# Landing each weight chunk in two halves: a two-layer transformer and a hybrid layer on one core

## What is computed

```python
def swiglu(x, w_gate_up, w_down):
    g, u = jnp.split(x @ w_gate_up, 2, axis=-1)
    return (jax.nn.silu(g) * u) @ w_down

# layer 0
y = short_conv_mixer(rms_norm(h, g0), conv_w_in, conv_w, conv_w_out)
h = h + rms_norm(y, post0)
h = h + rms_norm(swiglu(rms_norm(h, f0), w_gate_up[0], w_down[0]), fpost0)
# layer 1: k, v = shared_kv(h); dilated attention; the same feed-forward
# second block: x @ w_in, attention and pooling branches, w_out, conv feed-forward
```

## Time and profile before

| | us |
|---|---|
| median of 3 runs | 1239.92 |
| the profiled execution's own time | 1239.94 |
| its span | 1238.0 |
| PE busy | 1159.1 (94%) |
| DVE busy | 727.2 (59%) |
| ACT busy | 584.2 (47%) |
| all DMA, mean rate over the span | 156 GB/s |

### The profile page before, as it was taken

One profiled execution on the slowest core, in us unless ns is written; L12 is line 12 of the kernel. 1 busy time (PEld: TensorE's weight loads), 2 busy tenths in 40 slices (PEclk: granted clock), 3 DMA queues, 4 the chain that ended last, 5 costly groups with the idle time before them and its releaser, 6 DMA issues.

```text
span 1238.0 us, 17037 instructions
## 1 busy us (share of the span) xinstructions
PE 1159.1 (94%) x6724; PEld 1033.6 (83%) x6724; DVE 727.2 (59%) x940; ACT 584.2 (47%) x738; POOL 63.4 (5%) x49
## 2 busy tenths in 40 slices
PE   5998999989888999999988999999899998899998
PEld 5996777778888999999966777788898897899987
DVE  3865454455755565566555445455665564888862
ACT  4435534354545444554445534454534373566550
POOL 0110000000000000000000000000020020122310
PEclk8998999999999999999999999999999999999999
DMA  6554455666265554435233565766516353455662
GB/s 202 185 193 151 155 165 175 211 219 202 54 165 136 153 152 104 128 96 130 102 127 108 164 193 156 241 208 170 136 57 184 111 183 121 156 185 172 212 221 75
DMA packets 211330, 193.70 MB, mean 156 GB/s; under 512 B 5529, under 2 KB 186829, under 8 KB 211277
## 3 DMA queue, kind: packets, MB, share of 16 engines
q1 hardware_dynamic: 211277, 192.95, 50.8%
HBM read 191.88 MB, written 1.05 MB: 156 GB/s over the span
## 4 chain that ended last, share of the span: by engine, by line
PE 50%; DMA 17%; DVE 14%; ACT 9%; issue 7%; SPq 2%; ACTq 0%; DVEq 0%
DVE w_lo L1545 10%; DMA raw<-in_ffn_w_gate_up 7%; PE ps L570 6%; PE ps L572 6%; PE ps L571 6%; DMA raw<-in_ffn_w_down 4%; ACT w_hi L1117 4%; PE ps L695 3%; PE ps L697 3%; PE ps L696 3%; PE ps L620 3%; PE ps L621 3%; PE ps L622 3%; DMA raw<-in_w_q 3%; PE ps L726 2%
## 5 line engine op out<-in xcount | busy, mean ns | idle before, releaser
L1545 DVE TENSOR_TENSOR w_lo<-raw,w_hi 128x2048 fp32r<-128x2048 f32 (+2 forms) x157 | 404.5, 2588 | 156.4 <-ACT w_hi L1117 156.4
L1117 ACT ACTIVATE w_hi<-raw 128x2048 fp32r<-128x2048 f32 (+2 forms) x157 | 338.3, 2156 | 321.8 <-DMA raw<-in_ffn_w_gate_up 125.9
L570 PE MATMUL ps<-x_hi,w_hi 128*128 128x256 f32 x656 | 187.9, 286 | 5.0 <-DVE w_lo L1545 5.0
L571 PE MATMUL ps<-x_lo,w_hi 128*128 128x256 f32 x656 | 186.2, 284 | 0.0
L572 PE MATMUL ps<-x_hi,w_lo 128*128 128x256 f32 x656 | 186.1, 284 | 0.0
L620 PE MATMUL ps<-w_hi,x_hi 128*128 128x512 f32 (+1 forms) x368 | 146.1, 397 | 1.0 <-DVE w_lo L1545 0.7
L622 PE MATMUL ps<-w_hi,x_lo 128*128 128x512 f32 (+1 forms) x368 | 143.1, 389 | 0.0
L621 PE MATMUL ps<-w_lo,x_hi 128*128 128x512 f32 (+1 forms) x368 | 143.1, 389 | 0.0
L570 PEld LDWEIGHTS ps<-x_hi,w_hi 128*128 128x128 f32 x656 | 126.6, 193 | 5.5 <-DVE w_lo L1545 5.4
L571 PEld LDWEIGHTS ps<-x_lo,w_hi 128*128 128x128 f32 x656 | 126.7, 193 | 0.1
L572 PEld LDWEIGHTS ps<-x_hi,w_lo 128*128 128x128 f32 x656 | 126.5, 193 | 0.0
(11 more groups left out here) (218 smaller groups left out, 1738.3 us busy)
## 6 DMA issues: line engine op xcount, KB each, us to landing
raw<-in_ffn_w_gate_up SPq DMA_DIRECT2D x88, 512.0 KB, 4.9
raw<-in_w_kv SPq DMA_DIRECT2D x48, 512.0 KB, 6.4
raw<-in_w_up SPq DMA_DIRECT2D x22, 1024.0 KB, 5.1
raw<-in_conv_w_in SPq DMA_DIRECT2D x12, 1024.0 KB, 5.1
raw<-in_ffn_w_down SPq DMA_DIRECT2D x8, 1536.0 KB, 7.3
raw<-in_w_q SPq DMA_DIRECT2D x24, 512.0 KB, 5.2
raw<-in_ffn_w_down SPq DMA_DIRECT2D x8, 1280.0 KB, 6.0
raw<-in_w_in SPq DMA_DIRECT2D x10, 1024.0 KB, 5.5
```

The costliest lines, as they stand in the source:

```text
L570: nc.tensor.matmul(o, wh[:, k0 + k, c], hi[:, k, :], start=(k == 0), stop=False)
L571: nc.tensor.matmul(o, wh[:, k0 + k, c], low, start=False, stop=False)
L1117: nc.scalar.activation(w_hi[:, s, 0:size], raw[:, r, 0:size], ACT.Copy)\
L1545: nc.vector.tensor_tensor(w_lo[:, s, 0:size], raw[:, r, 0:size], w_hi[:, s, 0:size], ALU.subtract)\
```

## The change

`raw` keeps its size but has four places of half the size. Each chunk is cut by K tiles (8 into 4 and 4, 6 into 3 and 3, 5 into 3 and 2, 4 into 2 and 2). Each half has its own place, its own DMAs, its own semaphore, its own copy on ACT and its own subtraction on DVE. `hi_ready` and `lo_ready` count halves: the load of a half waits for DVE's subtraction of the same half of chunk n-2, and PE still waits for both halves of a chunk. Pieces that were one DMA become two, but for the four chunks of `branches`, whose two pieces are the two halves already. The memory of `raw`, the four places of `w_hi` and `w_lo`, PE's program and the order of the other work stay.

```diff
--- before.py
+++ after.py
@@ -68,8 +68,20 @@
     def size(self, j):
         return self.kts[j] * self.cols
 
+    def part(self, j, h):
+        mid = (self.kts[j] + 1) // 2
+        return (0, mid) if h == 0 else (mid, self.kts[j])
+
+    def part_pieces(self, j, i, h):
+        a, b = self.part(j, h)
+        cut = [(max(k0, a), min(k0 + kn, b), k0, c0, cw, src) for k0, kn, c0, cw, src in self.pieces(j, i)]
+        return [(lo - a, hi - lo, c0, cw, src[:, lo - k0:hi - k0, :]) for lo, hi, k0, c0, cw, src in cut if hi > lo]
+
     def n(self, j, i):
         return i * 4 + (self.n0 + j)
+
+    def n2(self, j, i):
+        return i * 8 + 2 * (self.n0 + j)
 
 
 def build(nc, a, out):
@@ -97,7 +109,7 @@
 
 
         SLOT = 3072
-        raw = at("raw", [P, 2, SLOT], F32)
+        raw = at("raw", [P, 4, SLOT // 2], F32)
         w_hi = at("w_hi", [P, 4, SLOT], F32R)
         w_lo = at("w_lo", [P, 4, SLOT], F32R)
         h = at("h", [P, 2, D], F32)
@@ -243,20 +255,22 @@
             Phase("down2", 8, DOWN_KT, 512, down_pieces(down_w[2]), banked=False),
         ]
         by_name = {}
-        chunk_at, landed, per_slot = [], [], [0, 0]
+        chunk_at, landed, per_slot = [], [], [0, 0, 0, 0]
         for ph in phases:
             ph.n0 = len(chunk_at)
             by_name[ph.name] = ph
             for l in range(ph.count):
                 real = not (ph.empty_last and l % 4 == 3)
+                r = len(chunk_at) % 2 * 2
                 if real:
-                    per_slot[len(chunk_at) % 2] += 16 * len(ph.pieces(l % 4, l // 4))
-                landed.append(per_slot[len(chunk_at) % 2])
+                    for h_ in range(2):
+                        per_slot[r + h_] += 16 * len(ph.part_pieces(l % 4, l // 4, h_))
+                landed.append(per_slot[r:r + 2])
                 chunk_at.append((ph, l) if real else None)
         TOTAL = len(chunk_at)
 
 
-        raw_in = [sem(f"raw_in{s}") for s in range(2)]
+        raw_in = [sem(f"raw_in{s}") for s in range(4)]
         hi_ready = sem("hi_ready")
         lo_ready = sem("lo_ready")
         product_done = sem("product_done")
@@ -435,13 +449,18 @@
                 n, i = n + 4 * i, 0
             eng.wait_ge(emptied[n % 4], i + (used[n] + 1))
 
-        def raw_level(ph, j, i):
+        def raw_slot(ph, j, h_):
+            r = (ph.n0 + j) % 2 * 2 + h_
+            a, b = ph.part(j % 4, h_)
+            return r, raw[:, r, 0:(b - a) * ph.cols]
+
+        def raw_level(ph, j, i, h_):
 
             n = ph.n0 + j
             if isinstance(i, int):
-                return landed[n + 4 * i]
-            step = landed[n + 4] - landed[n]
-            return i * step + landed[n]
+                return landed[n + 4 * i][h_]
+            step = landed[n + 4][h_] - landed[n][h_]
+            return i * step + landed[n][h_]
 
         def next_chunk(ph, l):
 
@@ -487,11 +506,13 @@
         def _(sp):
             def load(ph, j, i):
                 n = ph.n(j, i)
-                if not isinstance(i, int) or n >= 2:
-                    sp.wait_ge(lo_ready, n - 1)
-                s = (ph.n0 + j) % 2
-                for k0, kn, c0, cw, src in ph.pieces(j, i):
-                    sp.dma_start(slot(raw, s, ph)[:, k0:k0 + kn, c0:c0 + cw], src).then_inc(raw_in[s], 16)
+                for part in range(2):
+                    if not isinstance(i, int) or n >= 2:
+                        sp.wait_ge(lo_ready, ph.n2(j, i) + (part - 3))
+                    r, flat_raw = raw_slot(ph, j, part)
+                    dst = flat_raw.rearrange("p (k c) -> p k c", c=ph.cols)
+                    for k0, kn, c0, cw, src in ph.part_pieces(j, i, part):
+                        sp.dma_start(dst[:, k0:k0 + kn, c0:c0 + cw], src).then_inc(raw_in[r], 16)
 
             sp.dma_start(ident[:], a["c_ident"]).then_inc(x_in, 16)
             for t in range(2):
@@ -548,7 +569,7 @@
         @block.tensor
         def _(pe):
             def ready(ph, j, i, bank=True):
-                pe.wait_ge(lo_ready, ph.n(j, i) + 1)
+                pe.wait_ge(lo_ready, ph.n2(j, i) + 2)
                 n = ph.n0 + j + (4 * i if isinstance(i, int) else 0)
                 if bank and (used[n] > 0 or not isinstance(i, int)):
 
@@ -763,7 +784,7 @@
                     if n == 0:
                         pe.wait_ge(v_stored, 8)
                         pe.wait_ge(o_split, 6)
-                    pe.wait_ge(lo_ready, w.n0 + j + 1)
+                    pe.wait_ge(lo_ready, w.n2(j, 0) + 2)
                     ins = tokens(w, j, t, range(4), Y_BANK[3][t][j], x_hi, x_lo, first=True)
                     if t == 1:
                         ins.then_inc(product_done, 1)
@@ -1109,13 +1130,15 @@
         def _(act):
             def split(ph, j, i):
 
-                n, s, r = ph.n(j, i), (ph.n0 + j) % 4, (ph.n0 + j) % 2
-                act.wait_ge(raw_in[r], raw_level(ph, j, i))
-                if not isinstance(i, int) or n >= 4:
-                    act.wait_ge(product_done, n - 3)
-                size = ph.size(j)
-                nc.scalar.activation(w_hi[:, s, 0:size], raw[:, r, 0:size], ACT.Copy)\
-                    .then_inc(hi_ready, 2 if ph.empty_last and j == 2 else 1)
+                n, s = ph.n(j, i), (ph.n0 + j) % 4
+                for part in range(2):
+                    r, src = raw_slot(ph, j, part)
+                    act.wait_ge(raw_in[r], raw_level(ph, j, i, part))
+                    if part == 0 and (not isinstance(i, int) or n >= 4):
+                        act.wait_ge(product_done, n - 3)
+                    a, b = ph.part(j, part)
+                    nc.scalar.activation(w_hi[:, s, a * ph.cols:b * ph.cols], src, ACT.Copy)\
+                        .then_inc(hi_ready, 3 if part and ph.empty_last and j == 2 else 1)
 
             def high(bi, t, r, k):
 
@@ -1538,12 +1561,15 @@
 
             def split(ph, j, i):
 
-                n, s, r = ph.n(j, i), (ph.n0 + j) % 4, (ph.n0 + j) % 2
+                s = (ph.n0 + j) % 4
                 two = ph.empty_last and j == 2
-                dve.wait_ge(hi_ready, n + (2 if two else 1))
-                size = ph.size(j)
-                nc.vector.tensor_tensor(w_lo[:, s, 0:size], raw[:, r, 0:size], w_hi[:, s, 0:size], ALU.subtract)\
-                    .then_inc(lo_ready, 2 if two else 1)
+                for part in range(2):
+                    r, src = raw_slot(ph, j, part)
+                    dve.wait_ge(hi_ready, ph.n2(j, i) + (part + 1))
+                    a, b = ph.part(j, part)
+                    c = slice(a * ph.cols, b * ph.cols)
+                    nc.vector.tensor_tensor(w_lo[:, s, c], src, w_hi[:, s, c], ALU.subtract)\
+                        .then_inc(lo_ready, 3 if part and two else 1)
 
             def low(bi, t, r, k):
```

## The result

The changed kernel takes 1198.11 us (median of 4 runs, 1197.05 to 1202.7), beside it the kernel before 1239.11 (4 runs): ratio 0.968, 95% interval 0.965 to 0.972, so it is faster by 2.8 to 3.5%. The forecast was 1201.0, the range 1191 to 1218. The profiled execution took 1197.06 us with a span of 1195.1; against the 1238.0 of before that is 42.9 us less.

The account below looks back on a forecast made before the run. Up stages were held by an 11.94 us loop through one landing place, PE needing 11.33. Waits 33.5 plus clock 6.0 less instructions 0.8 gave 38.7 off 1239.9: 1201 us, range 1191 to 1218.

Parts of the forecast that it names:

- The loop: Up stages, one unit through a landing place: 11.94 us falls to 10.3, under PE's 11.33, so PE becomes the bound.
- 1 transposes: PE's waits at L684 for mid_t in gate and up units: 16.0 us of 18.0 saved.
- 2 L620: PE's four waits at L620 for late chunks: 3.0 us of 3.4 saved.
- 3 attention, first steps: Waits at L695, L740 and L747 behind L1298 in attention's first steps: 8.0 us of 8.4 saved.
- 4 L654: Waits at the boundaries, behind DVE's split, including the end of down1: 2.4 us of 8.5 saved.
- 5 L855: Wait behind ACT's split at 891.15 and a root that DVE waits for: 2.5 us of 5.5 saved.
- 7 L584: PE's wait for the first chunk: ACT ends 0.85 us sooner, at a halved clock, 0.4 us of 6.8 saved.
- clock, the nine stretches: PE's 3.4 us stretches at 0.50 after the first 20 us: three go, two shrink, 6.0 us saved.
- more instructions: Second copies and subtractions for 157 chunks: hidden except at seven places of 0.12 us each, costing 0.8 us.
- Halves land no sooner: Rival on landing: the second half still lands 4.90 us after issue, saving only 26 us, 1214; chance 0.18.
- Slower, the DMA queue: Rival in up0 and up1: eight 256 KB DMAs per unit make the queue the bound, 1260 us; chance 0.04.
- Waits move on: Rival: PE's other partners become late and halved clock returns elsewhere, costing 5 to 8 us; no separate chance given.

Follow-up runs that it names:

- experiment 3: The changed kernel, but ACT's first copy of a chunk waits until both halves have landed: 1218.72 us, ratio 0.985.
- 4: The changed kernel, but both halves' loads wait until both halves of the chunk two before are subtracted: 1214.32 us, ratio 0.982.
- 5: The kernel before, with only ACT's order in gate and up units changed, silu and hidden_high ahead of the second split: 1217.92 us, ratio 0.984.
- experiment 9: The changed kernel with silu and hidden_high moved ahead of the second split in ACT's body of up0 and up1: 1197.57 us, ratio 0.965.
- experiment 11: The changed kernel, but PE starts on the first half at five w_lo waits, at two also on a pair's first chunk alone: 1184.24 us, ratio 0.958.
- experiment 6: The changed kernel, but in up0 and up1 both halves are asked for together and ACT waits for both: 1229.41 us, ratio 0.993.
- experiment 2: The kernel before, each load cut into DMAs of half the K tiles, with one wait for both, copy and subtraction whole: 1254.22 us, ratio 1.015.
- 7: The changed kernel, but up0 and up1 fully as in the kernel before, with whole chunks and uncut DMAs: 1215.16 us, ratio 0.980.
- 8: The kernel before with halves in up0 and up1 alone, every other phase as before: 1218.12 us, ratio 0.982.

## Why the prediction was right, by its steps

**The loop**: forecast 2.35 + 0.71 + 4.0 + 0.10 + 1.05 + 2.10 = 10.3 us; the rows above give 2.36 for the two halves (mean 1.218 each, starting 1.14 apart), 0.76 to the last DMA, 4.18 to the copy, 1.06 and 2.12: 10.48. The one estimate in it was the landing: 4.0 and 0.10 to the copy, 4.18 measured for the two; PE became the bound, as said. Experiments 3 and 4 show that both overlaps were needed for that, 5 that the loop's path went through the silu.

**The sum**, each with 0.16 per wait as in the prediction, forecast and measured:

| term | forecast | measured, from the waits before and after |
|---|---|---|
| 1 transposes | 16.0 | 15.1 - 0.5 + 16 x 0.16 = 17.2 |
| 2 L620 | 3.0 | 3.4, none left |
| 3 attention, first steps | 8.0 | 3.1 + 2.3 + 2.4 + 4 x 0.16 = 8.4 |
| 4 L654 | 2.4 | 2.3 + 2 x 0.16 = 2.6 |
| 5 L855 | 2.5 | 2.0 |
| 6 L747 behind L1391 | 1.2 | 0.6 |
| 7 L584 | 0.4 | 2.3 |
| clock, the nine stretches | 6.0 | 3.9 |
| clock, first 20 us | not counted | 1.5 |
| more instructions | -0.8 | -0.2 |
| sum | 38.7 | 41.7 of 42.9 |

The clock's number: after the first 20 us the windows at 0.50 hold 29.8 us of PE's busy time before and 22.0 after (the sums of the view of windows over all of them), and half of the 7.8 is saved; in the first 20 us they hold 2.9 before and none after. Of the five stretches that were to go or shrink, those at 102, 351, 795 and 935 us are gone; the one after L855 stayed. One at 609.2 is new, behind a wait of 1.82 us at L761, and that in the last boundary is 6.8 long instead of 3.4. The wait at L761 is no longer than it was before the change (also 1.82, at 639.14, with the clock at 1.00 after it), so the record does not show why the clock fell there. The -0.2 is what L591 and L625 grew by; more is hidden in what the other rows already count. That the total came so close is in part luck: the waits gave 3.0 more than forecast and the start's clock 1.5, the nine stretches 2.1 less.

**The step that was mis-sized** is term 7. I had counted half a copy at ACT's end (0.85) and put it down to 0.4. What I overlooked stands in the timelines of ACT, before and after:

```profile
11.38 1.91 ACT L1117 ACTIVATE w_hi<-raw 128x2048 fp32r<-128x2048 f32 x1 [2.26 <-DMA raw<-in_conv_w_in]
```

```profile
8.88 2.23 ACT L1140 ACTIVATE w_hi<-raw 128x1024 fp32r<-128x1024 f32 x2
```

The first half of the first chunk is there when ACT asks for it, 2.5 us before the one DMA of 1 MB was. The second half sets the pace, as the chains of work show, before and after (start, us, what):

```profile
3.07 8.29 DMA raw<-in_conv_w_in
```

```profile
3.53 6.50 DMA raw<-in_conv_w_in
```

It lands at 10.03 where the whole chunk landed at 11.36. That is 1.33 us sooner, which I had left out, and ACT's last copy is 0.85 shorter (1.06 for 1.91), which I had in it: together the 2.2 by which PE starts sooner. The first product starts at 15.07 instead of 17.18, after PE has stood for 4.46 us instead of 6.80. The clock of the first 20 us changed as well. Before, after, and in experiment 9:

```profile
13.30:20.10 6.80, 2.92 (x13) 2.92 (x14) 6.05 (x8) 6.42 (x13) 0.00 (x0) 0.50 0.46 126
```

```profile
13.30:20.10 6.80, 5.03 (x29) 5.04 (x30) 6.17 (x12) 5.83 (x10) 0.00 (x0) 1.00 0.72 203
```

```profile
13.30:20.10 6.80, 4.43 (x20) 4.43 (x21) 6.76 (x13) 5.87 (x11) 0.00 (x0) 0.57 0.69 192
```

0.50 before and 1.00 after. The prediction had left this stretch out of its clock, and the shorter wait does not explain it: in experiment 9 PE stood for the same 4.46 us and was granted 0.57, in experiment 11 for 3.46 and 0.75, and in experiment 6 it stood for 5.42 and kept 1.00. So the 1.5 us in the table are no gain that the change is shown to bring, and the other clock row, read from one execution of each kernel, carries some of the same doubt.

**The rivals.** *Halves land no sooner*: false, 256 KB land in 4.2 where 512 KB took 4.9; this is the page's issue part after, then before:

```profile
raw<-in_ffn_w_gate_up SPq DMA_DIRECT2D x176, 256.0 KB, 4.2
```

```profile
raw<-in_ffn_w_gate_up SPq DMA_DIRECT2D x88, 512.0 KB, 4.9
```

*Slower, the DMA queue*: eight DMAs fit in a unit of 11.4 us, but the mechanism exists. In the unit shown it has its place in the issues and not in the bytes: experiment 2 lost 16 us, and there the last DMA goes out 1.1 us later and lands 0.5 sooner. In the change the later issues are hidden, since the first half's DMAs go out while DVE subtracts the second. The rule of the Trainium skill ("DMA: Bandwidth & Descriptors", Measured), to batch to 1 MiB, points the way that experiment 2 went; it does not hold for the change itself, where a smaller DMA is released and used sooner. The 2.6 us estimated from that page for 256 KB ("Anatomy of one DMA", a fit to DMAs issued from GpSimd, where these are issued from SP) stand against 4.2 measured with others in flight, and eight of them take 11.4 us or less and not 21, so they overlap. *Waits move on* happened in small, as halved clock that came back elsewhere: the stretch at 609.2 gave back nearly 1.8 us. DVE was 743.6 and ACT 603.2 us busy, where near 745 and near 615 were forecast; in the last up projection DVE stood at 18.27 of 20 us, beside 18.39 before.

**What the expectations had wrong**: experiment 2 by 4 us; experiment 3 by 8 us, since I counted the copy's overlap and not that the landing is longer; experiment 6 by 3 us, its edit changed more than it was read to; experiment 11 by 4 us to the fast side, about what the halved clock gave it. Of the last 1.2 us of the 42.9, 0.9 are small waits that the table leaves out: 0.4 at L794, which is gone, 0.1 at L707, and 0.1 and one of the two times at L632, with 0.16 for each that went. Not settled: whether the 0.3 to 0.6% by which 7 and 8 together exceed the whole is overlap or noise, and what moves the halved clock about.

## What to carry to other kernels

Where a landing place limits a loop (free, issue, land, copy, subtract), halves of it pay if each is released, landed and used on its own; cutting the DMAs alone cost 1.5%. A wait of the bottleneck engine for a small intermediate is to be followed back along the in-order engines until something else than their order ends it: here that led to a landing, and moving two instructions ahead of the waiting one gave half of the whole gain without touching memory. When data comes in halves, look at what the last consumer waits for: starting it on less was worth another 1%. Halves alone are shown for 2.1 us of that; 6.2 lay where it had waited for a pair of chunks, and much of the rest was the clock.

## What was not expected of the hardware

Half the bytes cut a landing by far less than half: 4.9 to 4.2 us from 512 to 256 KB, and, for the chunks of the last up projection, 5.1 to 4.5 from 1024 to 512 KB. In the unit of experiment 2 that is shown, DMAs issued on one queue go out 0.55 us apart, and that spacing, and not the bytes, was the cost of cutting them. Copies and subtractions could be cut again, 628 more instructions, for 3 us in all by the medians. And after the same 4.46 us of standing at the start, TensorE ran on at the 2.4 GHz level in one kernel and fell to the 1.2 GHz level, from about 15 us on, in another.
